# Later feed-forward blocks and three of four down pairs by seven products of quadrants, with GpSimd summing the weight quadrants

## The chip, the cores and the metric

The kernel is one program on one core of a Trainium2 chip. The engines named here are TensorE (PE in the rows, with PEld for its weight loads), VectorE (DVE), ScalarE (ACT), GpSimd (POOL) and the sync engine (SP), which issues most DMAs. The metric is the device time of one execution in microseconds (us). Three runs of the kernel before took 1226.31, 1227.39 and 1228.52 us, median 1227.39.

## What is computed

Two stacked model blocks over 256 tokens of width 1024, all in float32. The first block is feed-forward, then a mixer (differential attention beside an mLSTM), then a second feed-forward. The second block has a gated delta layer and a sparse attention layer. The change touches only the two feed-forward parts and what shares engines with them:

```python
u = modulate(rmsnorm(h, g_ff1), sh1, sc1)             # u: 256 x 1024
h = h + 0.5 * gt1 * ((silu(u @ w1_gate) * (u @ w1_up)) @ w1_down)   # 2816 hidden columns
...
u = modulate(rmsnorm(h, g_ff2), sh3, sc3)
h = h + 0.5 * gt3 * ((silu(u @ w2_gate) * (u @ w2_up)) @ w2_down)
mods = silu(c) @ w_ada + b_ada                        # shifts, scales, gates; also ada_w of block two
```

## The kernel before

Activations lie transposed: `U` and `H` are 128 partitions by 8 chunks of width by 256 tokens. Weights come through a ring `W` of four slots of 2 MB, filled by SP in the order in which they are used. `f1` and `f2` are the two feed-forward parts. The hidden columns of one part are 22 chunks of 128, in 11 blocks of two chunks. For one chunk, `t_gate` issues 16 matrix products (gate and up, 8 chunks of width each) of a 128x128 weight tile with 256 moving columns. In the profile each float32 product appears as two MATMUL records (and two weight loads), so a block of two chunks is 64 records. ScalarE takes the tanh (`s_gate`), VectorE makes the silu and the product (`v_gate`) into `actT`.

The down projection runs over four pairs of output chunks: `t_down` issues 44 products per pair (88 records of 256 columns); the last pair is done in two halves of 128 tokens, so that the next norm can start on half 0. `v_residual` adds the result to `H`.

The first four blocks of `f1` are done as their weights arrive (`t_first_gate`); `t_gate` handles blocks 4 to 10 of `f1`, and all of `f2`. In `f2` block 0 runs in two halves of tokens, since its input `U` comes out of the norm `n3` half by half: `v_root` (reciprocal), `v_normed` (four products H x rstd) and `s_normed` (eight activations) per half.

Beside it VectorE works off the modulation vectors: `v_mod_column` multiplies a 128x1024 tile of the ada weights with the silu of c and sums it (the CUSTOM_DVE rows, ISA in the program's order). Groups of four such tiles come through the same ring `W`, one group per block (`v_ada_blocks`), and `v_ada_mods` adds the bias. Two small extras sit early in `f1`: `t_lambda` and `t_bias` on TensorE; the row of biases is copied by VectorE (`v_bias`) and written to memory by GpSimd (`p_bias`). GpSimd otherwise adds squares for the norms and does nothing during the feed-forward blocks.

Every engine runs its list in order; waits are on counters of the other engines. The order of each list is the order of the calls in `tensor`, `vector`, `scalar`, `gpsimd` and `sync`. A `ring` hands out buffers in turn; `open` waits until the buffer was closed by its last user.

## Time and profile before

| | |
|---|---|
| runs | 1226.31, 1227.39, 1228.52 us |
| profiled execution, span from first to last instruction | 1226.5 us |
| PE busy | 1215.9 us, 99% |
| PEld busy | 1056.1 us, 86% |
| DVE, ACT, POOL busy | 500.7, 297.4, 80.4 us |
| mean granted clock of TensorE | 0.998 |
| chain that ended last | PE 95%, DVE 2%, ACT 1%, DMA 1% |
| HBM | 236.8 MB read, 197 GB/s over the span |

No time of the profiled execution as a whole is recorded beside its span; the span lies 0.9 us under the median of the runs and is taken as its time. A busy share says how long an engine had an instruction in it. Matmuls are pipelined, so that their recorded durations overlap; the pace is read from the starts of neighbouring groups.

### The profile page before, as it was taken

Reading aid. Unit: us, or ns where it says so; the run is one execution under the profiler, and the core shown is the slowest. Engines: PE = TensorE matmul, PEld = TensorE weight load, DVE = VectorE, ACT = ScalarE, POOL = GpSimd, SP = SyncE. Lnnn points to the kernel's source line nnn. Section 1 sums busy time; section 2 is a strip of 40 time slices with the busy share of each in tenths; the row PEclk is TensorE's granted clock in tenths of the full one; section 3 lists DMA queues with packets and bytes.
Section 4 is the critical chain, followed back from the end, with each engine's and each line's share of the span. In section 5 each row is a group of like instructions: output and inputs, shape, how many; then the busy total and the mean of one; then the engine's idle time right before and its main releaser. Section 6 shows DMA issues by size and latency. Waiting matters only on the chain.

```text
span 1226.5 us, 17258 instructions
## 1 busy us (share of the span) xinstructions
PE 1215.9 (99%) x7122; PEld 1056.1 (86%) x7122; DVE 500.7 (41%) x1442; ACT 297.4 (24%) x855; POOL 80.4 (7%) x103
## 2 busy tenths in 40 slices
PE   9999999999999999999999999999999999999997
PEld 7888888996678888889988888898888998888887
DVE  4434440072027533351445442037765322157632
ACT  2110000042124434100300001034424421146542
POOL 0000000000012000011000000030000310000111
PEclk9999999999999999999999999999999999999999
DMA  9968873572475455566888885358242563543311
GB/s 347 336 236 295 308 248 124 205 275 95 151 234 155 174 206 197 183 236 223 278 307 309 309 290 187 105 203 280 78 122 80 187 215 112 153 122 104 104 70 35
DMA packets 163263, 241.52 MB, mean 197 GB/s; under 512 B 13057, under 2 KB 111551, under 8 KB 163184
## 3 DMA queue, kind: packets, MB, share of 16 engines
q1 hardware_dynamic: 155296, 230.45, 55.2%
q10 hardware_dynamic: 6784, 5.74, 1.6%
q0 software_dynamic: 1104, 4.22, 1.0%
q8 instruction: 56, 0.92, 0.3%
q14 instruction: 23, 0.19, 0.0%
HBM read 236.82 MB, written 4.62 MB: 197 GB/s over the span
## 4 chain that ended last, share of the span: by engine, by line
PE 95%; DVE 2%; ACT 1%; DMA 1%; POOL 0%; issue 0%; DVEq 0%; ACTq 0%
PE ps L189 93%; PE ps L192 2%; ACT U L195 1%; DVE tmpB L204 0%; DMA bias_row<-rows 0%; DMA arena<-bias_row 0%; DVE rstd L216 0%; ACT arena L195 0%; ACT tmpC L195 0%; DVE U L198 0%; POOL arena L198 0%; POOL tmpC L198 0%; DVE arena L216 0%; ACT rstd L195 0%; DVE arena L198 0%
## 5 line engine op out<-in xcount | busy, mean ns | idle before, releaser
L189 PE MATMUL ps<-U,slots 128*128 128x256 f32 (+2 forms) x3424 | 700.0, 365 | 0.2 <-DVE arena L198 0.2
L189 PEld LDWEIGHTS ps<-U,slots 128*128 128x128 f32 (+1 forms) x3424 | 601.4, 190 | 78.9 <-issue 5.0
L189 PE MATMUL ps<-arena,slots 128*128 128x256 f32 (+1 forms) x1840 | 324.1, 338 | 0.0
L189 PEld LDWEIGHTS ps<-arena,slots 128*128 128x128 f32 x1840 | 292.5, 191 | 30.1 <-issue 1.8
L207 DVE CUSTOM_DVE_ANT_0 slots<-slots,tmpA 128x1024 f32<-128x1024 f32 x104 | 123.2, 1230 | 5.1 <-DMA slots<-in_w_adaT 4.8
L195 ACT ACTIVATE tmpC<-ps 128x256 f32<-128x256 f32 (+3 forms) x95 | 38.4, 409 | 341.0 <-PE ps L189 334.8
L195 ACT ACTIVATE arena<-ps 128x512 f32<-128x512 f32 (+3 forms) x116 | 50.5, 459 | 153.2 <-PE ps L189 148.9
L204 DVE SCALAR_TENSOR_TENSOR tmpC<-tmpC,ps 128x256 f32<-128x256 f32 (+1 forms) x46 | 18.8, 409 | 149.3 <-ACT tmpC L195 149.3
L195 ACT ACTIVATE tmpC<-H 128x512 f32<-128x512 f32 (+2 forms) x32 | 15.8, 506 | 237.9 <-DVE H L204 195.8
L204 DVE SCALAR_TENSOR_TENSOR H<-ps,sm,H 128x256 f32<-128x256 f32 (+1 forms) x32 | 11.9, 413 | 136.9 <-PE ps L189 136.9
L195 ACT ACTIVATE arena<-arena,st 128x128 f32<-128x128 f32 (+2 forms) x128 | 48.5, 405 | 31.9 <-DVE st L201 31.9
L189 PE MATMUL ps<-arena 128*128 128x128 f32 (+7 forms) x544 | 55.5, 295 | 0.0
L189 PEld LDWEIGHTS ps<-arena 128*128 128x128 f32 (+2 forms) x544 | 47.4, 173 | 8.5 <-issue 4.3
L204 DVE SCALAR_TENSOR_TENSOR tmpB<-arena,hw,tmpB 128x256 f32<-128x256 f32 x96 | 46.5, 485 | 3.4
L195 ACT ACTIVATE U<-U,mods,sm 128x128 f32<-128x128 f32 (+1 forms) x72 | 30.3, 494 | 46.1 <-DVE sm L204 32.1
L195 ACT ACT_TABLE_LOAD x24 | 30.8, 1283 | 10.1 <-DVE tmpB L204 6.4
L207 DVE CUSTOM_DVE_ANT_0 arena<-ps,arena 128x128 f32<-128x128 f32 (+2 forms) x96 | 21.9, 290 | 25.0 <-PE ps L189 24.8
L198 POOL TENSOR_TENSOR arena<-tmpC 128x512 f32<-128x512 f32 x6 | 7.6, 1263 | 350.3 <-ACT tmpC L195 350.3
L204 DVE SCALAR_TENSOR_TENSOR arena<-tmpC,ps 128x512 f32<-128x512 f32 (+1 forms) x18 | 11.3, 631 | 42.0 <-ACT tmpC L195 41.9
L189 PE MATMUL ps<-slots,U 128*128 128x512 f32 x64 | 28.1, 592 | 0.0
L219 DVE COPY arena<-ps 64x256 f32<-64x256 f32 (+2 forms) x16 | 7.3, 457 | 48.9 <-PE ps L189 48.7
L201 DVE TENSOR_SCALAR arena<-arena,st,gates 128x128 f32<-128x128 f32 (+1 forms) x96 | 26.3, 345 | 0.6
(162 smaller groups left out, 747.4 us busy)
## 6 DMA issues: line engine op xcount, KB each, us to landing
slots<-in_w_adaT SPq DMA_DIRECT2D x14, 2048.0 KB, 7.8
slots<-in_w_in SPq DMA_DIRECT2D x14, 2048.0 KB, 9.2
slots<-in_w_down SPq DMA_DIRECT2D x16, 1408.0 KB, 6.6
slots<-in_w_gate SPq DMA_DIRECT2D x18, 1024.0 KB, 5.2
slots<-in_w_up SPq DMA_DIRECT2D x18, 1024.0 KB, 7.9
slots<-in_ada_w1T SPq DMA_DIRECT2D x6, 2048.0 KB, 7.9
slots<-in_ada_w2T SPq DMA_DIRECT2D x6, 2048.0 KB, 8.2
slots<-in_a_in_w SPq DMA_DIRECT2D x6, 2048.0 KB, 10.3
```

The lines of the kernel that those rows point to most:

```text
L189: return Nothing() if self.e is None else self.e.matmul(*a, **k)
L192: return Nothing() if self.e is None else self.e.transpose(*a, **k)
L195: return Nothing() if self.e is None else self.e.activation(*a, **k)
L198: return Nothing() if self.e is None else self.e.tensor_tensor(*a, **k)
L201: return Nothing() if self.e is None else self.e.tensor_scalar(*a, **k)
L204: return Nothing() if self.e is None else self.e.scalar_tensor_tensor(out=o, in0=i0, scalar=s, in1=i1, op0=op0, op1=op1)
L207: return Nothing() if self.e is None else self.e.tensor_tensor_reduce(*a)
L219: return Nothing() if self.e is None else self.e.tensor_copy(*a)
```

## The change

The change computes blocks 5 to 10 of `f1`, blocks 1 to 10 of `f2`, and down pairs 0 to 2 of both parts, by the Winograd form of Strassen's scheme: each matrix product is cut into quadrants (width, weight columns and tokens in halves), and seven products of quadrants, of 128 moving columns each, take the place of eight. That needs sums of quadrants of the weights and of the activations beforehand, and sums of products afterwards.

- `t_gu` on TensorE: seven products p1, p2, p6, p5, p7, p3, p4, each for gate and up, 4 chunks of width, 128 tokens: 56 products of 128 columns for a block in place of 32 of 256. `t_dn`: 7 x 11 = 77 in place of 44 for a pair.
- `p_t` on GpSimd: the four weight sums t1 to t4 of a block, 1024 elements per partition each. t1, t2, t4 go to a ring of two sets (`TG`); t3 overwrites a quadrant of the weight slot. p6 waits for t2, p7 for t3, p4 for t4.
- `p_dn_t` on GpSimd: three sums of 1408 elements for a down pair; the fourth (`v_dn_t1`) is VectorE's.
- `v_su` and `v_sd` on VectorE: the four sums of the activations (of `U`, once for each part, and of `actT`).
- Running sums: ScalarE copies the products' partial sums out of PSUM (s1, u2, s5, u3, c21); VectorE adds (`v_gu`, `v_dn`); then tanh, silu and product on a whole block at once (`s_gu_tanh`, `v_gu_act`).
- The ada tiles no longer go through `W` but through a ring `AR` of four single tiles of 0.5 MB in the arena, loaded by `fetch_chunk`: three a block for most blocks, four for each of the down pairs. The weights of `f1` block b+1 (`f2` block b+2) stand on SP's queue beside the tiles of block b.
- `p_bias` stays at the head of GpSimd's list, ahead of the first `p_t`; `v_bias` now comes right after `v_gate(9)`. The squares' sums move from the arena to `ABT`; rope's load moves into the norm `n2`. `tmpB` and `tmpC` become parts of one tile `tmps`, the PSUM banks parts of one tensor `ps`.

```diff
             for b in range(4, 11):
-                fetch("ada", b)
                 if b < 10:
                     fetch("f1 gu", b + 1)
-            for h in range(8):
-                fetch("f1 dn", h)
+                for g, c in CHUNKS["f1"].get(b, ()):
+                    fetch_chunk(g, c)
+            for p in range(4):
...
+            fetch("f2 gu", 0)
+            fetch("f2 gu", 1)
+            e.wait_ge(*pe.at("pb", 3))
             for b in range(11):
-                fetch("f2 gu", b)
-                fetch("ada", 18 + b)
-            for h in range(8):
-                fetch("f2 dn", h)
+                for g, c in CHUNKS["f2"].get(b, ()):
+                    fetch_chunk(g, c)
+                if b < 9:
+                    fetch("f2 gu", b + 2)
...
+        AR = ring(*[arena[:, 5632 + 1024 * i:6656 + 1024 * i] for i in range(4)])
+        CHUNKS = {"f1": {}, "f2": {}}
+        for f, g0, counts in (("f1", 4, {4: 3, 5: 3, 6: 3, 7: 3, 8: 2, 9: 2}),
+                              ("f2", 18, {0: 3, 1: 4, 2: 3, 3: 3, 4: 3, 5: 3, 6: 3, 7: 3, 8: 3})):
...
+        SETS = [(psum[:, i:i + 2, :], psum[:, i + 2:i + 4, :]) for i in (4, 0)]
+        Q = ring(*SETS)
...
+        TG = ring(*[arena[:, 9728 + 3072 * i:12800 + 3072 * i].rearrange("p (t n k c) -> p t n k c", t=3, n=2, k=4) for i in range(2)])
...
+        def v_su(e, f, tag):
...
+            a11, a12, a21, a22 = (U[:, 4 * k:4 * k + 4, HALF[h]] for h in range(2) for k in range(2))
+            e.tensor_tensor(SU[0], a21, a22, ALU.add).then_inc(*dve.up())
+            e.tensor_tensor(SU[2], a11, a21, ALU.subtract).then_inc(*dve.up())
+            e.wait_ge(*dve.now())
+            e.tensor_tensor(SU[1], SU[0], a11, ALU.subtract).then_inc(*dve.up())
+            e.wait_ge(*dve.now())
+            e.tensor_tensor(SU[3], a12, SU[1], ALU.subtract).then_inc(*dve.up("su", f))
+        def p_t(e, f, b):
+            t, free = TG.open(f, b)
+            for x in free:
+                e.wait_ge(*x)
+            w = gu_block(f, b)
+            e.wait_ge(*arrived(f + " gu", b))
+            e.tensor_tensor(t[:, 0], w[:, :, 0:4, P:T], w[:, :, 0:4, 0:P], ALU.subtract).then_inc(*pool.up(f, "t1", b))
+            e.wait_ge(*pool.at(f, "t1", b))
+            e.tensor_tensor(t[:, 1], w[:, :, 4:8, P:T], t[:, 0], ALU.subtract).then_inc(*pool.up(f, "t2", b))
+            e.tensor_tensor(w[:, :, 0:4, P:T], w[:, :, 4:8, P:T], w[:, :, 0:4, P:T], ALU.subtract).then_inc(*pool.up(f, "t3", b))
+            e.wait_ge(*pool.at(f, "t2", b))
+            e.tensor_tensor(t[:, 2], w[:, :, 4:8, 0:P], t[:, 1], ALU.subtract).then_inc(*pool.up(f, "t4", b))
+        def t_gu(e, f, b):
+            (A, C2), free = Q.open(f, b)
+            for x in free:
+                e.wait_ge(*x)
+            w, t = gu_block(f, b), TG.buf(f, b)
...
+            e.wait_ge(*dve.at("su", f))
+            e.wait_ge(*pool.at(f, "t2", b))
+            e.wait_ge(*act.at(f, "s1", b))
+            for n in range(2):
+                i = product(A[:, n, 0:P], t[:, 1, n], SU[1], False)
...
+            e.wait_ge(*pool.at(f, "t3", b))
+            e.wait_ge(*act.at(f, "u2", b))
+            for n in range(2):
+                i = product(A[:, n, 0:P], w[:, n, 0:4, P:T], SU[2], False)
+            i.then_inc(*pe.up(f, "p7", b))
...
+            W.close([pe.now(), pool.at(f, "t4", b)], f + " gu", b)
+            e.wait_ge(*pool.at(f, "t4", b))
+            e.wait_ge(*act.at(f, "u3", b))
+            for n in range(2):
+                i = product(A[:, n, 0:P], t[:, 2, n], U[:, 4:8, HALF[1]], False)
+            i.then_inc(*pe.up(f, "p4", b))
+            TG.close([pe.now()], f, b)
...
+            e.activation(E[:, :, 1, :], A, ACT.Copy).then_inc(*act.up(f, "u2", b))
...
+            if b - 1 >= (5 if f == "f1" else 1):
+                e.wait_ge(*dve.at(f, "c22", b - 1))
+            e.wait_ge(*pe.at(f, "p7", b))
+            e.activation(FG, A, ACT.Copy).then_inc(*act.up(f, "u3", b))
+            e.wait_ge(*pe.at(f, "p4", b))
+            e.activation(x_[:, 1, :, 0, :], A, ACT.Copy).then_inc(*act.up(f, "c21", b))
+        def v_gu(e, f, b):
+            (A, C2) = Q.buf(f, b)
+            E, x_ = EG.buf(f, b), XG.buf(f, b)
+            e.wait_ge(*act.at(f, "u2", b))
+            e.wait_ge(*act.at(f, "s5", b))
+            e.wait_ge(*pe.at(f, "p3", b))
+            e.tensor_tensor(x_[:, 0].rearrange("p n j t -> p n (j t)"), C2[:, :, 0:T], E.rearrange("p n j t -> p n (j t)"), ALU.add).then_inc(*dve.up(f, "c1", b))
+            e.wait_ge(*act.at(f, "u3", b))
+            e.tensor_tensor(x_[:, 1, :, 1, :], x_[:, 1, :, 1, :], FG, ALU.add).then_inc(*dve.up(f, "c22", b))
+        def s_gu_tanh(e, f, b):
+            E, x_ = EG.buf(f, b), XG.buf(f, b)
+            th = E.rearrange("p h j t -> p h (j t)")
+            e.wait_ge(*dve.at(f, "c22", b))
+            e.wait_ge(*act.now())
+            e.activation(th, x_[:, :, 0].rearrange("p h j t -> p h (j t)"), ACT.Tanh, scale=0.5).then_inc(*act.up(f, "th", b))
+        def v_gu_act(e, f, b):
+            E, x_ = EG.buf(f, b), XG.buf(f, b)
+            th = E.rearrange("p h j t -> p h (j t)")
+            e.wait_ge(*act.at(f, "th", b))
+            e.stt(th, th, 1.0, x_[:, :, 0].rearrange("p h j t -> p h (j t)"), ALU.add, ALU.mult).then_inc(*dve.up())
+            e.wait_ge(*dve.now())
+            to = actT[:, 2 * b:2 * b + 2, :].rearrange("p j (h t) -> p h j t", h=2)
+            e.tensor_tensor(to, E, x_[:, :, 1], ALU.mult).then_inc(*dve.up())
+            dve.mark(f, "act", 2 * b)
+            dve.mark(f, "act", 2 * b + 1)
+            EG.close([dve.now()], f, b)
+            XG.close([dve.now()], f, b)
...
+        def v_sd(e, f, k0, k1):
+            a11, a12, a21, a22 = (actT[:, 11 * k + k0:11 * k + k1, HALF[h]] for h in range(2) for k in range(2))
+            s1, s2, s3, s4 = (SD[:, n, k0:k1, :] for n in range(4))
+            e.wait_ge(*dve.at(f, "act", 10 + k1))
+            e.tensor_tensor(s1, a21, a22, ALU.add).then_inc(*dve.up())
+            e.tensor_tensor(s3, a11, a21, ALU.subtract).then_inc(*dve.up())
+            e.wait_ge(*dve.now())
+            e.tensor_tensor(s2, s1, a11, ALU.subtract).then_inc(*dve.up())
+            e.wait_ge(*dve.now())
+            e.tensor_tensor(s4, a12, s2, ALU.subtract).then_inc(*dve.up())
...
+        def v_dn_t1(e, f, p):
+            lo, hi = dn_of(f, p)
+            e.wait_ge(*(pe.at(f, "p4", 9) if p == 0 else pe.at(f, "p4", 10) if p == 1 else pe.at(f + " dn", "p4", 0)))
+            e.wait_ge(*arrived(f + " dn", 2 * p))
+            e.tensor_tensor(TD[3 * p % 4], lo[:, :, P:T], lo[:, :, 0:P], ALU.subtract).then_inc(*dve.up(f + " dn", "t1", p))
+        def p_dn_t(e, f, p):
+            lo, hi = dn_of(f, p)
+            t1, t2, t4 = (TD[(3 * p + n) % 4] for n in range(3))
+            e.wait_ge(*dve.at(f + " dn", "t1", p))
+            e.wait_ge(*arrived(f + " dn", 2 * p + 1))
+            if p:
+                e.wait_ge(*pe.at(f + " dn", "p5", p - 1))
+            e.tensor_tensor(t2, hi[:, :, P:T], t1, ALU.subtract).then_inc(*pool.up(f + " dn", "t2", p))
+            e.tensor_tensor(lo[:, :, P:T], hi[:, :, P:T], lo[:, :, P:T], ALU.subtract).then_inc(*pool.up(f + " dn", "t3", p))
+            e.wait_ge(*(pe.at(f + " dn", "p6", p - 1) if p else pe.at(f, "p4", 10)))
+            e.wait_ge(*pool.at(f + " dn", "t2", p))
+            e.tensor_tensor(t4, hi[:, :, 0:P], t2, ALU.subtract).then_inc(*pool.up(f + " dn", "t4", p))
...
+            product(A[:, 0:P], lo[:, :, 0:P], actT[:, 0:11, HALF[0]], True, 0).then_inc(*pe.up(n, "p1", p))
+            e.wait_ge(*arrived(n, 2 * p + 1))
+            product(C2[:, 0:P], hi[:, :, 0:P], actT[:, 11:22, HALF[0]], True, 11).then_inc(*pe.up(n, "p2", p))
+            e.wait_ge(*dve.at("sd", f))
+            e.wait_ge(*pool.at(n, "t2", p))
+            e.wait_ge(*act.at(n, "s1", p))
+            product(A[:, 0:P], t2, SD[:, 1], False).then_inc(*pe.up(n, "p6", p))
+            product(C2[:, P:T], t1, SD[:, 0], False).then_inc(*pe.up(n, "p5", p))
...
+            for p in range(3):
+                t_dn(e, f, p)
+            for x in free_of(Q, 1):
+                e.wait_ge(*x)
+            t_down(e, f, 3, 0)
+            t_down(e, f, 3, 1, amid={(1, 0): first_sums})
...
+            t_gate(e, "f1", 8, "n1")
+            t_gate(e, "f1", 9, "n1")
+            t_lambda(e)
+            t_bias(e)
+            for x in free_of(S, 1) + free_of(X):
+                e.wait_ge(*x)
+            t_gu(e, "f1", 5)
+            for x in free_of(L) + free_of(S):
+                e.wait_ge(*x)
+            for b in range(6, 11):
+                t_gu(e, "f1", b)
+            t_downs(e, "f1", "n2")
...
+        def v_gu_blocks(e, f, b0):
+            for b in range(b0, 11):
+                if b > b0:
+                    v_gu_act(e, f, b - 1)
+                chunks = CHUNKS[f].get(b, [])
+                v_ada_chunks(e, chunks[:2])
+                if b == 10:
+                    v_sd(e, f, 0, 9)
+                    v_dn_t1(e, f, 0)
+                v_ada_chunks(e, chunks[2:])
+                v_gu(e, f, b)
+            v_gu_act(e, f, 10)
+            v_sd(e, f, 9, 11)
...
+            v_su(e, "f1", "n1")
+            v_gate(e, "f1", 8)
+            v_gate(e, "f1", 9)
+            v_bias(e)
+            v_ada_chunks(e, CHUNKS["f1"][4])
+            v_gu_blocks(e, "f1", 5)
...
         def gpsimd(e):
             p_bias(e)
+            for b in range(5, 11):
+                p_t(e, "f1", b)
+            for p in range(3):
+                p_dn_t(e, "f1", p)
...
+            e.wait_ge(*pe.at("sums", "n3", 1))
+            e.wait_ge(*pool.now())
+            for b in range(1, 11):
+                p_t(e, "f2", b)
+            for p in range(3):
+                p_dn_t(e, "f2", p)
```

The order on two engines. GpSimd's list, from its first work on, before (names: `bias_row` is memory, `tmpC` and `arena` scratch):

```order
L225 DMA bias_row<-tmpB 16x384
L198 ISA
L198 TENSOR_TENSOR arena<-tmpC 128x512
L198 TENSOR_TENSOR arena<-arena,tmpC 128x512
L198 TENSOR_TENSOR arena<-arena 128x256
```

And now, for the first block with seven products and the start of the third (`slots` are weights, `s_products` is TensorE's counter):

```order
L225 DMA bias_row<-tmps 16x384 [waits s_vector_results]
L198 ISA
L198 TENSOR_TENSOR arena<-slots 128x1024 [waits s_slot0]
L198 TENSOR_TENSOR arena<-slots,arena 128x1024 [waits s_pool_results]
L198 TENSOR_TENSOR slots<-slots 128x2x4x128
L198 TENSOR_TENSOR arena<-slots,arena 128x1024 [waits s_pool_results]
...
L198 TENSOR_TENSOR arena<-slots 128x1024 [waits s_slot2,s_products]
```

The sums of the weights stand between the DMA of the bias row and the work that was GpSimd's first; from the third block on the first of four waits for TensorE.

VectorE's list for a block of `f1` before: two `v_gate` (here the second) and four ada tiles (ISA rows):

```order
L204 SCALAR_TENSOR_TENSOR tmpC<-tmpC,ps 128x256 [waits s_scalar_results]
L198 TENSOR_TENSOR arena<-tmpC,ps 128x256 [waits s_vector_results]
L207 ISA slots,mods<-slots,tmpA 128x1024 [waits s_slot0]
L207 ISA mods 128x1
L207 ISA slots,mods<-slots,tmpA 128x1024
L207 ISA mods 128x1
```

And now, around block 6: `v_gu(5)`, `v_gu_act(5)`, then three ada tiles, the first shown whole:

```order
L198 TENSOR_TENSOR tmps<-ps,tmps 128x512 [waits s_products,s_scalar_results]
L198 TENSOR_TENSOR tmps<-tmps,rstd 128x2x128 [waits s_scalar_results]
L204 SCALAR_TENSOR_TENSOR tmps<-tmps 128x512 [waits s_scalar_results]
L198 TENSOR_TENSOR arena<-tmps 128x2x2x128 [waits s_vector_results]
L207 ISA arena,mods<-arena,tmpA 128x1024 [waits s_ada_chunk2]
L207 ISA mods 128x1
```

Before, each `v_gate` row has one input in PSUM (`ps`). Now three of the four rows of a block take both inputs from SBUF, and the ada tiles stand between the activation of one block and the sums of the next.

## Rows read from the trace of the kernel before

**Rows 1.** The page: busy time, and the chain that ended last by engine.

```profile
PE 1215.9 (99%) x7122; PEld 1056.1 (86%) x7122; DVE 500.7 (41%) x1442; ACT 297.4 (24%) x855; POOL 80.4 (7%) x103
PE 95%; DVE 2%; ACT 1%; DMA 1%; POOL 0%; issue 0%; DVEq 0%; ACTq 0%
```

**Rows 2.** Busy time in windows; window, length, engines (instructions), clock, DMA share, GB/s.

```profile
89.00:103.00 14.00, 14.00 (x65) 11.94 (x65) 6.40 (x13) 0.48 (x3) 0.00 (x0) 1.00 0.86 300
229.00:249.00 20.00, 20.00 (x178) 19.90 (x177) 3.87 (x9) 3.74 (x9) 2.90 (x4) 1.00 0.56 211
```

**Rows 3.** Timeline of TensorE: start, length, instruction, shape, records.

```profile
24.47 1.89 PE L189 MATMUL ps<-U,arena 128*128 128x256 f32 x8
26.20 5.34 PE L189 MATMUL ps<-U,slots 128*128 128x256 f32 x24
...
88.76 14.08 PE L189 MATMUL ps<-U,slots 128*128 128x256 f32 x64
...
172.69 71.88 PE L189 MATMUL ps<-arena,slots 128*128 128x256 f32 x396
...
244.63 5.08 PE L189 MATMUL ps<-arena,slots 128*128 128x128 f32 x44
249.54 3.74 PE L189 MATMUL ps<-U,slots 128*128 128x128 f32 x32
253.11 0.39 PE L189 MATMUL ps<-arena,cst 128*128 128x128 f32 x2
...
738.79 7.50 PE L189 MATMUL ps<-arena,slots 128*128 128x256 f32 x34
```

**Rows 4.** Groups of GpSimd by shape: count, busy us, mean ns, idle before.

```profile
L198 POOL TENSOR_TENSOR arena<-tmpC 128x512 f32<-128x512 f32 x6 | 7.6, 1263 | 350.3 <-ACT tmpC L195 350.3
L198 POOL TENSOR_TENSOR tmpC<-tmpC 128x128 f32<-128x128 f32 x16 | 7.3, 455 | 54.6 <-ACT tmpC L195 54.6
```

**Rows 5.** Timeline of GpSimd, 539 to 551 us.

```profile
539.09 2.18 POOL L198 TENSOR_TENSOR arena<-arena,tmpB 128x512 f32<-128x512 f32 x1 [121.88 <-DVE tmpB L204]
543.94 2.18 POOL L198 TENSOR_TENSOR arena<-arena,tmpB 128x512 f32<-128x512 f32 x1 [2.67 <-DVE tmpB L204]
550.85 1.26 POOL L198 TENSOR_TENSOR arena<-arena,tmpB 128x512 f32<-128x512 f32 x1 [4.72 <-DVE tmpB L204]
```

**Rows 6.** Timeline of VectorE in the same stretch.

```profile
538.93 1.22 DVE L207 CUSTOM_DVE_ANT_0 slots<-slots,tmpA 128x1024 f32<-128x1024 f32 x1
540.07 2.28 DVE L207 CUSTOM_DVE_ANT_0 slots<-slots,tmpA 128x1024 f32<-128x1024 f32 x1
...
545.04 1.10 DVE L198 TENSOR_TENSOR mods<-mods,vec 128x4 f32<-128x4 f32 x1
```

**Rows 7.** Timeline, 955 to 960 us: GpSimd, and VectorE with an input in PSUM.

```profile
955.17 4.96 POOL L198 TENSOR_TENSOR H<-H,arena 128x512 f32<-128x512 f32 x4
...
958.99 0.69 DVE L198 TENSOR_TENSOR arena<-arena,ps 128x512 f32<-128x512 f32 x1 [2.05 <-PE ps L189]
```

**Rows 8.** Timeline, 103 to 105 us: the bias row.

```profile
104.14 0.54 DVE L219 COPY tmpB<-ps 16x384 f32<-16x384 f32 x1
104.99 0.70 POOL L225 DMA_DIRECT2D bias_row<-tmpB  x1 [104.55 <-DVE tmpB L219]
```

**Rows 9.** Timeline, 586 to 600 us: the norm ahead of the second feed-forward.

```profile
589.02 1.07 POOL L225 DMA_DIRECT2D bias_rows<-bias_row  x1
589.46 7.31 PE L189 MATMUL ps<-U,slots 128*128 128x128 f32 x64
590.06 0.95 DVE L216 RECIPROCAL rstd<-rstd 128x128 f32<-128x128 f32 x1 [4.20 <-ACT rstd L195]
591.05 1.43 DVE L198 TENSOR_TENSOR U<-H,rstd 128x256 f32<-128x256 f32 x4
591.51 3.19 ACT L195 ACTIVATE U<-U,mods,sm 128x128 f32<-128x128 f32 x8 [1.48 <-DVE U L198]
596.98 3.28 PE L189 MATMUL ps<-U,slots 128*128 128x128 f32 x27 [0.21 <-DVE arena L198]
```

**Rows 10.** Window at the end of the program, with TensorE mostly idle.

```profile
1216.00:1226.00 10.00, 4.06 (x35) 3.68 (x33) 4.65 (x8) 2.20 (x8) 0.00 (x0) 0.81 0.34 105
```

268 lines of the change are left out of this document (212 added, 56 removed).

## The prediction

> **What bounds the kernel now.** First the page: TensorE is busy 99% of the span and makes up 95% of the chain that ended last; VectorE is busy 41%, GpSimd 7% [rows 1]. So time is won only by less work on TensorE, as long as nothing else becomes late. Then the windows: in a 14 us stretch of gate/up blocks TensorE has no gap, VectorE works 6.4 us, GpSimd nothing; in a stretch of 128-column products the weight loads are as full as the products, 19.90 of 20.00 us [rows 2]. Then the timeline, for the pace: 8 records of 256 columns from 24.47 to 26.20, 216 ns each; 76 records of 128 columns from 244.63 to 253.11, 111.6 ns each, not 108 [rows 3]. Last, the timelines of GpSimd and VectorE side by side, because the change gives both much work at once: there stands the price that the diff does not show [rows 5, 6].
>
> **TensorE's work.** A gate/up block is 64 records at 216 ns = 13.8 us before and 112 at 111.6 ns = 12.5 us after; 16 blocks save 16 x 1.32 = 21.2 us. A down pair is 88 x 216 ns = 19.0 us before and 154 x 111.6 ns = 17.2 us after; 6 pairs save 10.9 us. Together 32 us of TensorE time: that is all there is to win.
>
> **GpSimd's work.** 128 elements take 455 ns and 512 take 1263 ns [rows 4], so 2.10 ns an element and 0.19 us fixed. A sum of 1024 elements is then 2.34 us, four of them 9.4 us a block; a sum of 1408 is 3.15 us, three of them 9.5 us a pair. Alone, this fits under 12.5 and 17.2 us.
>
> **The two engines exclude each other.** At 539.09 GpSimd starts a sum of 512 elements while VectorE is in an ada tile. It takes 2.18 us in place of 1.26, and ends 1.20 us after VectorE's tile ended at 540.07 [rows 5, 6]. VectorE's next tile, issued at 540.07, takes 2.28 us in place of 1.22: it started only when GpSimd was through, near 541.13. A sum of 4 elements at 545.04 takes 1.10 us, also behind a sum of GpSimd. The next GpSimd sum, with VectorE free, takes 1.26 us again. Where VectorE has one input in PSUM nothing happens: at 958.99 it takes 0.69 us inside 4.96 us of GpSimd sums that keep 1.24 us each [rows 7]. So VectorE's instructions with two SBUF inputs and GpSimd's sums take turns, each for its whole transfer. Behind these rows stands the Trainium skill, "SBUF — State Buffer", terms and port section: the shared port pair is an exclusive lock held for the full instruction, and the loser fully blocks. By that rule the two loads add up; by shared bandwidth they would hide behind each other, which would give the first rival's time. The trace agrees with the lock.
>
> The hold of a sum of 512 was 540.07 to 541.13, 1.06 to 1.1 us, which is 2.1 ns an element; I take 2.2 us for 1024 and 3.0 for 1408. VectorE holds for 1.08 us per tile (538.93 to 540.07, less 0.06) and about 1.05 ns an element otherwise.
>
> **One block after.** GpSimd 4 x 2.2 = 8.8 us. VectorE with two SBUF inputs: three ada tiles 3.24, c22 of 256 elements 0.27, the two activation steps of 512 elements 1.07, bias sums 0.05: 4.6 us (the sum c1 has PSUM in it and is free). Total 13.4 us of turns. Some ten changes of hand come on top; no row prices them apart, the bounds are 0 (the next is queued) and 0.15 us (GpSimd's fixed part less what overlaps). I take 0.05, an estimate near the lower end, since the engine that waits is already issued: 13.9 us a block, between 13.4 and 14.9. That is above TensorE's 12.5 and level with today's 13.8. What TensorE saves in a block, it waits.
>
> **f1, blocks 5 to 10.** GpSimd's list begins with the bias row's DMA, which waits for VectorE's copy (104.14 to 104.68 today, DMA at 104.99 for 0.70) [rows 8]. In the new order the copy comes after `v_gate(9)`, about 90.3 us, so the sums start at 91.6, while TensorE is ready for block 5 at 89.6 and reaches p6 3.6 us later without t2. From 91.6 on: 24 sums x 2.2 = 52.8; VectorE's turns 16 tiles x 1.08 = 17.3, activations and c22 of five blocks 6.7, four sums of 1152 elements ahead of the downs 4.8, the first down sum 1.5, together 30.3; some 60 changes 3.0. Sum 86.1, so the last t4 is there at 177.7; p4 and the tail of TensorE 2.1: 179.8. Today the downs start at 172.7 [rows 3]. **+7.1 us.**
>
> **f2's norm.** `p_t` of block 1 may start once the norm's sums are taken, and its weights are there. GpSimd is free at 590.1, one us ahead of the first of four normed products of VectorE (591.05 to 592.48), which TensorE's half 1 of block 0 waits for [rows 9]. Each product holds 0.27 us and takes two SBUF inputs. t1 runs to 592.4, then the products alternate with t2, t3, t4: the fourth ends at 592.4 + 0.3 + 3 x (2.2 + 0.3 + 0.1) = 600.5, the last activation of `U` 0.9 later, the product that needs it at 601.8, where it is at 596.8 now. TensorE had only 0.21 us of idle time there. What is queued behind the blocked product is all of VectorE's list, and behind that the activations. **+4.8 us.** Cover that is gone: none. If GpSimd comes 2 us later, it is a little less; bounds 0 and 8.
>
> **f2, blocks 1 to 10.** 10 x 13.9 = 139.0 against 738.8 - 600.6 = 138.2 [rows 3, 9] (596.98 plus the 32 records left of block 0). **+0.8 us**, bounds -4 and +11.
>
> **Downs.** Three pairs of 17.2 are 51.6 us. At the start p6 of pair 0 needs the sums of `actT` with the last block in them: two activation steps and four small sums of VectorE, each of which can meet one of GpSimd's three sums of 3.0 us; that is 9 us of holds and 1.5 of VectorE's, after a tanh 1 us behind p4, while TensorE has p1 and p2, 4.9 us, to do. It waits 10.5 - 4.9 = 5.6 us. Sum 57.2 against 3 x 19.0 = 57.0. Later pairs: 9.0 + 4 tiles 4.3 + 1.5 + 1.5 = 16.3 us of turns, under 17.2. **About 0**, bounds -5 (no wait) and +6, for both parts together -10 and +12.
>
> Moved at no price: v_su (2.1 us of VectorE, hidden behind blocks 0 and 4), the ada tiles as such (same count), ScalarE's five copies of about 0.4 us a block, rope's load.
>
> **Sum.** 7.1 + 4.8 + 0.8 + 0.2 = +12.9 us: 1226.5 -> 1239.4 for the span, and 0.9 more against the median of the runs: **1240 us**. Its own range, from the bounds of a change of hand and of the downs, is 1229 to 1256.
>
> **Rivals.**
> 1. *The port is no limit.* GpSimd and VectorE mostly miss each other. Then TensorE's 32 us come, less about 3 us at block 5: 1198 us. For it: 9.4 us of GpSimd in 12.5. Against it: the three contended rows, all full waits [rows 5, 6].
> 2. *The turns fit.* The holds are as I say, but half of VectorE's turns fall into GpSimd's own pauses (waits for `TG`, for itself), and a block takes 12.9: f1 +2, norm +3, blocks of f2 -9, downs -3: -7, 1220 us. For it: two sets of t buffers are a block of lead. Against it: the turns alone are 13.4.
> 3. *VectorE's chain becomes the bound* (slower than my forecast, and on the other side of before for certain). tanh of block b waits for c22 of b, the next activation for tanh, the tiles come behind it, c22 of b+1 behind those, and u2, on which p7 waits, is behind tanh on ScalarE. Own time of this chain is 7.5 us; where each of four GpSimd sums stops it for its whole hold, 7.5 + 8.8 = 16.3 us a block, 2.4 more than above. It decides once VectorE is more than about 6 us behind TensorE. With 2.4 us on some ten of 16 blocks: 1264 us. SP's list makes it worse: the weights of a later block stand behind tiles whose buffers VectorE must free. A code load of GpSimd's (the ISA row ahead of its first sum) would also fall on the path now; no row prices it.
> 4. *TensorE slows down in its gaps.* With TensorE busy 4.06 of 10 us the granted clock was 0.81 of full, so part of that stretch was at 1.2 GHz [rows 10]. The waits at block 5, at the norm and at the downs are of 5 us each; if each costs 2 us more, 1248 us. It only widens the range.
>
> That the change does not do what it says is no rival of weight: the program's order has the seven products.
>
> **How the numbers follow.** My forecast 0.50 (with rival 4), rival 1 0.12, rival 2 0.18, rival 3 0.20. A difference under 0.2%, 2.5 us, cannot be told from none. Faster: 0.12 + 0.17 + 0.03 of the forecast's lower end = 0.32; same 0.08; slower 0.60. The range for 8 in 10 leaves out most of rival 1 and the far end of rival 3: 1204 to 1264.
>
> **What would show it.** GpSimd's sums of 1024 recorded with a mean near 3 us, not 2.35, and ada tiles well over 1.23: the lock. Block starts in f2 13 to 15 us apart, with TensorE idle before p7 or p6: the turns bound. First p_t at 91 to 92 us, not earlier. The four normed products near 590 spread over 8 us. PEld and PE at 111 to 112 ns a record within products. Wrong it would be if tiles stay at 1.23 us beside GpSimd, if blocks are 12.5 us apart, or if TensorE waits for DMA rather than for `arena` or `tmps`.

## The result, and the profile after

Four runs of the changed kernel took 1258.99 to 1261.04 us, median 1260.55, beside 1227.43 for the kernel before: ratio 1.0266, 95% interval 1.0253 to 1.0279. It is slower by 33 us where 13 were forecast. The profiled execution spans 1258.6 us (1226.5 before).

The page after, busy time and the chain that ended last, against [rows 1]; then TensorE's waits: engine that waits, for whom, total us, times, longest.

```profile
PE 1205.9 (96%) x8286; PEld 1084.5 (86%) x8286; DVE 685.7 (54%) x1496; ACT 330.6 (26%) x943; POOL 322.4 (26%) x185
...
PE 77%; DVE 15%; POOL 2%; ACT 2%; DMA 2%; issue 2%; DVEq 0%; ACTq 0%; POOLq 0%
```

```profile
PE ps L189 <- ACT tmps L195: 20.5, 10, 7.4
PE ps L189 <- DVE arena L198: 11.8, 5, 5.2
PE ps L189 <- POOL arena L198: 7.8, 3, 7.1
PE ps L189 <- ACT U L195: 3.3, 4, 1.3
```

VectorE has come onto the path (15% of the chain). It gained 185 us of busy time; with GpSimd's sums made free (experiment 1) the same 1496 instructions take 552.6 us, so 133 of these are waiting inside an instruction. TensorE's four waits sum to 43.4 us; in the kernel before the same kinds come to 1.5.

Now the groups by shape of GpSimd and VectorE (count, busy us, mean ns, idle before).

```profile
L198 POOL TENSOR_TENSOR arena<-slots,arena 128x1024 f32<-128x1024 f32 x32 | 90.2, 2819 | 1.3
L198 POOL TENSOR_TENSOR slots<-slots 128x1024 f32<-128x1024 f32 x16 | 44.5, 2778 | 0.0
```

```profile
L207 DVE CUSTOM_DVE_ANT_0 arena<-arena,tmpA 128x1024 f32<-128x1024 f32 x88 | 135.0, 1574 | 22.4 <-DMA arena<-in_w_adaT 19.6 <-DMA arena<-in_ada_w1T 2.6
L198 DVE TENSOR_TENSOR arena<-tmps 128x512 f32<-128x512 f32 x16 | 35.0, 2190 | 0.6
L204 DVE SCALAR_TENSOR_TENSOR tmps<-tmps 128x512 f32<-128x512 f32 x16 | 28.4, 1772 | 21.4 <-ACT tmps L195 21.4
L198 DVE TENSOR_TENSOR tmps<-tmps,rstd 128x256 f32<-128x256 f32 x16 | 27.8, 1740 | 0.0
L198 DVE TENSOR_TENSOR tmps<-ps,tmps 128x512 f32<-128x512 f32 x16 | 10.9, 683 | 16.1 <-PE ps L189 16.1
```

A sum of 1024 takes 2.8 us, not 2.34. The activation's two steps of 512 elements take 1.77 and 2.19 us; the one of the same size with an input in PSUM keeps 0.68. That is the lock of [rows 5, 6] against [rows 7], now all through both feed-forward parts.

The ledger by stage, from block and pair starts on TensorE's timeline:

| stage | before | after | change | forecast |
|---|---|---|---|---|
| up to the end of f1's blocks | 172.7 | 183.1 | +10.4 | +7.1 |
| f1 down pairs 0 to 2 | 57.0 | 60.6 | +3.5 | +0.2 |
| f2 norm and block 0 | 11.1 | 18.9 | +7.8 | +4.8 |
| f2 blocks 1 to 10 | 138.2 | 145.0 | +6.8 | +0.8 |
| f2 down pairs 0 to 2 | 57.0 | 60.3 | +3.3 | +0.2 |

The forecast has 57.2 against 57.0 us for the pairs of each part; its sum entered 0.2 for both together, where 0.4 follows. The first row hides a head start. In this execution the row of eight products that starts at 24.47 in [rows 3] starts at 22.39, and block 5 with its first products at 87.43, where 89.6 was forecast:

```profile
87.43 3.84 PE L189 MATMUL ps<-U,slots 128*128 128x128 f32 x32
```

In the experiments, which change nothing on TensorE ahead of this point, block 5 starts between 87.2 and 89.7. That is a difference between executions, and without it the first row would be some +12.5.

From the same starts the length of each of the 16 blocks follows. Seven take 12.5 us, four 13.3 to 13.8, and five 17.6 to 22.6: blocks 5 and 8 of f1, blocks 1, 4 and 9 of f2. The waits are few and long.

Three places in rows. First f1 block 5, all engines on the timeline (start, length, instruction, what the idle time before it ended with).

```profile
89.30 1.21 DVE L207 CUSTOM_DVE_ANT_0 arena<-arena,tmpA 128x1024 f32<-128x1024 f32 x1
89.34 5.66 POOL L198 TENSOR_TENSOR arena<-slots 128x1024 f32<-128x1024 f32 x1
...
90.44 1.21 DVE L207 CUSTOM_DVE_ANT_0 arena<-arena,tmpA 128x1024 f32<-128x1024 f32 x1
...
91.59 1.21 DVE L207 CUSTOM_DVE_ANT_0 arena<-arena,tmpA 128x1024 f32<-128x1024 f32 x1
...
92.84 2.18 DVE L198 TENSOR_TENSOR mods<-mods,vec 128x4 f32<-128x4 f32 x1
...
95.08 3.27 POOL L198 TENSOR_TENSOR arena<-slots,arena 128x1024 f32<-128x1024 f32 x1
...
98.40 6.40 PE L189 MATMUL ps<-ABT,arena 128*128 128x128 f32 x32 [7.14 <-POOL arena L198]
```

GpSimd's first sum was issued at 89.34 and ended at 95.00. It takes 2.35 us when alone, so it ran only from about 92.7, when VectorE's row of tiles had ended; VectorE's sum of 4 elements at 92.84 then waited for it. TensorE waits 7.14 us for t2, and its 32 records after that take 6.40 us, where the same row elsewhere takes 3.74. Second, f1 block 8.

```profile
141.31 3.36 DVE L207 CUSTOM_DVE_ANT_0 arena<-arena,tmpA 128x1024 f32<-128x1024 f32 x1
143.54 3.32 POOL L198 TENSOR_TENSOR slots<-slots 128x1024 f32<-128x1024 f32 x1
...
147.40 2.04 DVE L198 TENSOR_TENSOR tmps<-tmps,rstd 128x256 f32<-128x256 f32 x1
149.47 0.63 ACT L195 ACTIVATE tmps<-tmps 128x512 f32<-128x512 f32 x1 [11.26 <-DVE tmps L198]
...
150.52 3.75 PE L189 MATMUL ps<-ABT,slots 128*128 128x128 f32 x16 [7.43 <-ACT tmps L195]
```

This is the third rival's chain: c22 late on VectorE (147.40), tanh behind it, u2 behind tanh on ScalarE, and p7 waits 7.43 us for u2. What makes c22 late stands ahead of it: three tiles of 3.36 us each, where a tile takes 1.22 alone, so each one waited for a whole sum. Third, the norm of f2, against [rows 9].

```profile
604.08 2.37 POOL L198 TENSOR_TENSOR arena<-slots 128x1024 f32<-128x1024 f32 x1
605.02 9.18 DVE L198 TENSOR_TENSOR U<-H,rstd 128x256 f32<-128x256 f32 x4
...
614.79 2.08 PE L189 MATMUL ps<-U,slots 128*128 128x128 f32 x8 [0.48 <-ACT U L195]
...
617.40 9.89 PE L189 MATMUL ps<-U,slots 128*128 128x128 f32 x64 [0.54 <-DVE arena L198]
...
617.79 4.38 DVE L198 TENSOR_TENSOR ABT<-U 128x512 f32<-128x512 f32 x2
```

The four normed products take 9.18 us in place of 1.43, each behind one of GpSimd's sums. The four sums of U meet GpSimd's sums too: they run from 617.79 to 625.66, 7.9 us where the prediction has 2.1 us of own time and no price, and p6 of block 1 then waits 1.96 us. Last, the clock: busy time in windows (window, length, PE, PEld, DVE, ACT, POOL, granted clock, DMA share, GB/s).

```profile
95.00:98.40 3.40, 0.00 (x0) 0.00 (x0) 2.49 (x4) 0.00 (x0) 3.32 (x2) 0.50 1.07 361
98.40:105.00 6.60, 6.60 (x36) 6.60 (x37) 1.04 (x2) 0.46 (x2) 6.60 (x3) 0.59 1.06 382
150.50:154.00 3.50, 3.48 (x16) 3.50 (x17) 3.31 (x6) 0.15 (x1) 0.00 (x0) 0.50 0.91 290
...
105.00:143.00 38.00, 37.47 (x335) 37.21 (x333) 31.86 (x20) 6.33 (x16) 37.69 (x14) 1.00 0.58 196
```

Within the waits the granted clock falls to 0.50, the level of 1.2 GHz, and the products after the wait run at it for a while before they are back at 2.4 GHz. Taking each group of records over its pace of 111.6 ns a record, the slow ones lose 7.9 us in f1 and 13.5 in f2, 21 us together. The mean over the span is 0.975 (0.998 before).

### The profile page after: what moved, and what is told of

Same layout as the page of the kernel before. It is cut to its first block, busy times and chain, and to the rows that moved or that the text cites. A ratio compares the mean times of both kernels' runs of the same rounds, so it can differ in the third digit from the quotient of the medians.

```text
span 1258.6 us, 20000 instructions
## 1 busy us (share of the span) xinstructions
PE 1205.9 (96%) x8286; PEld 1084.5 (86%) x8286; DVE 685.7 (54%) x1496; ACT 330.6 (26%) x943; POOL 322.4 (26%) x185
## 3 DMA queue, kind: packets, MB, share of 16 engines
q10 hardware_dynamic: 6784, 5.74, 1.6%
## 4 chain that ended last, share of the span: by engine, by line
PE 77%; DVE 15%; POOL 2%; ACT 2%; DMA 2%; issue 2%; DVEq 0%; ACTq 0%; POOLq 0%
PE ps L189 75%; DVE arena L207 5%; DVE arena L198 4%; DVE tmps L198 2%; DVE tmps L204 2%; PE ps L192 2%; POOL arena L198 2%; ACT tmps L195 1%; DMA arena<-in_ada_w1T 1%; DVE ABT L198 1%; ACT U L195 0%; DMA bias_row<-rows 0%; DMA arena<-bias_row 0%; DVE rstd L216 0%; ACT arena L195 0%
## 5 line engine op out<-in xcount | busy, mean ns | idle before, releaser
L189 PE MATMUL ps<-U,slots 128*128 128x256 f32 (+2 forms) x2912 | 543.4, 346 | 3.9 <-ACT U L195 3.3
L189 PEld LDWEIGHTS ps<-U,slots 128*128 128x128 f32 (+1 forms) x2912 | 469.9, 192 | 57.1 <-issue 5.4
L189 PE MATMUL ps<-arena,slots 128*128 128x128 f32 (+1 forms) x1840 | 272.6, 308 | 10.3 <-DVE arena L198 10.3
L195 ACT ACTIVATE tmps<-ps 128x256 f32<-128x256 f32 (+2 forms) x151 | 56.4, 381 | 350.9 <-PE ps L189 338.9
L207 DVE CUSTOM_DVE_ANT_0 arena<-arena,tmpA 128x1024 f32<-128x1024 f32 x88 | 135.0, 1574 | 22.4 <-DMA arena<-in_w_adaT 19.6
L198 POOL TENSOR_TENSOR arena<-slots,arena 128x1024 f32<-128x1024 f32 (+1 forms) x44 | 129.2, 2937 | 68.6 <-DVE arena L198 32.3
L189 PE MATMUL ps<-arena 128*128 128x128 f32 (+7 forms) x940 | 106.1, 293 | 1.0 <-DVE arena L198 1.0
L189 PE MATMUL ps<-ABT,arena 128*128 128x128 f32 (+5 forms) x752 | 86.1, 279 | 9.1 <-POOL arena L198 7.1
L189 PEld LDWEIGHTS ps<-ABT,arena 128*128 128x128 f32 (+3 forms) x752 | 76.7, 181 | 10.3 <-POOL arena L198 7.3
L198 POOL TENSOR_TENSOR slots<-slots 128x1024 f32<-128x1024 f32 (+1 forms) x22 | 63.8, 2901 | 0.0
```

Source lines behind the costliest of these rows:

```text
L189: return Nothing() if self.e is None else self.e.matmul(*a, **k)
L195: return Nothing() if self.e is None else self.e.activation(*a, **k)
L198: return Nothing() if self.e is None else self.e.tensor_tensor(*a, **k)
L207: return Nothing() if self.e is None else self.e.tensor_tensor_reduce(*a)
```

## The experiments

All ratios are against the kernel before, from runs on the same chip, with 95% intervals. The experiments ran on several chips, on which the kernel before took 1225.95 to 1227.9 us, so times of different experiments compare to about 2 us. The edits are shortened: counter increments, and the moves of buffers and waits that an edit brings with it, are left out. Unless said otherwise the edits are made to the changed kernel (1260.55 us).

**1. The sums cut to 1 of 128 columns.**

```diff
-e.tensor_tensor(t[:, 0], w[:, :, 0:4, P:T], w[:, :, 0:4, 0:P], ALU.subtract)
+e.tensor_tensor(t[:, 0, :, :, 0:1], w[:, :, 0:4, P:P + 1], w[:, :, 0:4, 0:1], ALU.subtract)
... (t2, t3, t4 and the down pairs' sums alike)
```

> GpSimd's weight sums of the gate/up blocks and of the down pairs are cut to 1 of every 128 columns (the weight sums are left out, so the products with sums work on stale numbers; every instruction, wait and DMA stays). Theory A (GpSimd and VectorE shut each other out, and all of TensorE's waits come from that): the waits of 5 to 7 us before p6 and p7 of blocks 5, 8, 4 and 9 go, the clock stays at 2.4 GHz through both stages, and TensorE's 32 us come through: 1226 + 1 - 32 = about 1196 us (1192 to 1204). Theory B (VectorE's chain c22, tanh, activation, tiles is too long by itself, or SP's list order starves the blocks): the gate/up blocks still take 14 us or more each and the time stays above 1225 us.

1201.01 us beside 1225.95 for the kernel before, ratio 0.979 (0.9771 to 0.981), as theory A said. TensorE's saving is real, the f1 downs take 51.6 us, and of the large waits one is left, 3.00 us at block 5 with 3 us of slow products behind it. Timeline of GpSimd there:

```profile
91.35 3.53 POOL L198 TENSOR_TENSOR arena<-slots 128x8 f32<-128x8 f32 x1
```

An addition of 8 elements takes 3.53 us: it ends at 94.88, just behind the last of VectorE's row of tiles. Theory B falls.

**2. Throwaway products in TensorE's waits.**

```diff
+fill(e, C2[:, 0, 384:512], w, FILL6.get((f, b), 0))        # before p6: f1 b5: 28, f2 b1: 10
 e.wait_ge(*dve.at("su", f))
...
+fill(e, Q.buf(f, b - 1)[0][:, 0, 384:512], w, FILL7[f, b]) # before p7: f1 b8: 28, f2 b4: 14, b9: 12
 e.wait_ge(*pool.at(f, "t3", b))
```

> Adds throwaway products on TensorE (128 x 128 x 128, into PSUM columns that nobody reads) just where TensorE waits: 28 before p6 of f1 block 5, 28 before p7 of f1 block 8, 10 before p6 of f2 block 1, 14 and 12 before p7 of f2 blocks 4 and 9, 12 in block 0 of f2, 20 before the 20th activation row in the downs of both parts. They shorten no wait; they keep TensorE busy in it. Theory C (of the 32 us that the changed kernel is behind, some 19 are products run at 1.2 GHz after a wait): granted clock over the span from 0.975 back to above 0.99, and 8 to 16 us faster than the changed kernel, 1244 to 1252 us. Theory D (the waits alone cost the time; TensorE's slower pace after them is absorbed by the next wait): no change or slower by what the fills overrun, 1260 to 1268 us.

1252.65 us, ratio 1.0216 (1.0192 to 1.0239), with more work on TensorE: 8 us faster than the changed kernel by the medians, 6 by the ratios. The four runs spread from 1250.72 to 1256.1. Mean granted clock 0.993. The timeline of TensorE:

```profile
100.65 3.84 PE L189 MATMUL ps<-ABT,arena 128*128 128x128 f32 x32 [0.91 <-POOL arena L198]
150.47 2.02 PE L189 MATMUL ps<-ABT,slots 128*128 128x128 f32 x16 [1.19 <-ACT tmps L195]
...
624.82 5.44 PE L189 MATMUL ps<-ABT,arena 128*128 128x128 f32 x32 [2.17 <-ACT tmps L195]
```

Behind the filled waits of f1 the products are back at 3.84 and 2.02 us (6.40 and 3.75 unfilled). The slow pace lost falls from 21.4 to 6.4 us. Where TensorE is the bound after the wait, this comes through: f1's blocks take 91.3 us (95.7), its downs 58.3 (60.6), 6.7 us together. In f2 it does not: p6 of block 1 starts 25.8 us after the norm's products in both kernels (599.02 to 624.82 here, 603.44 to 629.25 there), because VectorE's normed products and U sums, and the silu of c behind them, end no earlier. From there to the downs both take 138 us; where block 4's wait is filled, block 5 waits 3.14 us instead. In f2's downs the filler did not hold the clock: the 44 records behind the wait take 6.80 us (7.19 unfilled, 5.08 at full clock). Theory C holds for f1, theory D for f2's norm and blocks; for f2's downs this run does not decide.

**3. GpSimd starts f2's sums after the last normed product.**

```diff
-e.wait_ge(*pe.at("sums", "n3", 1))
+e.wait_ge(*dve.at("un", "n3", 3, 1))
```

> GpSimd's weight sums for f2 block 1 (and all behind them) start after the last normed product of VectorE instead of after the statistics' sums. Theory A (the sums shut VectorE out of its four normed products, U comes late): the stretch 603.4 to 622.3 of the changed kernel (18.9 us against 11.1 before) shrinks by 5 to 8 us; the sums of block 1 then end some 3 us later and p6 of block 1 may wait 2 to 5 us, so -2 to -7 us in all: 1253 to 1259 us. Rival (the late U comes from ScalarE's normed parts or from the clock): no change within 1 us.

1260.45 us, ratio 1.0268 (1.0249 to 1.0287): nothing gained, where theory A expected 2 to 7 us. The products take 1.43 us again, and the next work of VectorE with two SBUF inputs is hit in their place (timeline of VectorE and TensorE):

```profile
606.17 1.43 DVE L198 TENSOR_TENSOR U<-H,rstd 128x256 f32<-128x256 f32 x4
...
612.49 5.60 DVE L198 TENSOR_TENSOR ABT<-U 128x512 f32<-128x512 f32 x2
...
629.64 5.83 PE L189 MATMUL ps<-ABT,arena 128*128 128x128 f32 x32 [10.13 <-ACT tmps L195]
```

**4. A small operation of GpSimd's at the start of the program.**

```diff
+e.memset(pw[:, :], 1.0)
+e.tensor_tensor(pw[:, 0:8], pw[:, 8:16], pw[:, 8:16], ALU.add)
 p_bias(e)
```

> A memset and one addition of 8 columns on a tile of their own at the head of GpSimd's work, at the start of the kernel. Theory E (GpSimd's first sum at 89.34 took 5.66 us because its code was loaded in it for some 3.4 us): the first sum then takes 2.2 to 3 us in the place and TensorE's wait of 7.14 us before p6 of block 5 shrinks by 3 us or more, with the clock behind it 4 to 6 us: 1254 to 1257 us. Rival F (VectorE's back-to-back tiles keep the port until 92.7, GpSimd only waits for it): the first sum stays at 5 us or more and the time does not change.

1260.16 us, ratio 1.0276 (1.0256 to 1.0297), and the first sum still takes 5.74 us. An earlier operation of the same kind changes nothing, so theory E falls and rival F fits.

```profile
90.68 5.74 POOL L198 TENSOR_TENSOR arena<-slots 128x1024 f32<-128x1024 f32 x1
```

**5. VectorE's tiles cut to 8 of 1024 elements.**

```diff
-v_mod_column(e, AR.buf(g, c), mod_col(g) + c)
+e.tensor_tensor_reduce(w[:, 0:8], w[:, 0:8], CR[:, 0:8], 0.5, 0.0, ALU.mult, ALU.add, mods[:, col:col + 1])
```

> VectorE's modulation tiles are cut to 8 of 1024 elements in the feed-forward stages (their sums are left out, so the modulation is wrong; every DMA, wait and order stays). VectorE loses some 1.1 us for each of 31 tiles of f1 and 44 of f2 and no longer keeps GpSimd out with them. Theory A (GpSimd's sums and VectorE's tiles shut each other out, and the waits of 5 to 7 us come from it): nearly the same as the run with narrow sums, 1198 to 1210 us. Rival G (of VectorE's work it is not the tiles but its activations, U sums and normed products that meet the sums, or SP's order of the weights): gate/up blocks 5 to 10 of f1 speed up only to 90 us and f2 stays above 160 us: 1235 to 1250 us.

1231.01 us, ratio 1.0032 (1.002 to 1.0045). The answer lies between: the tiles carry 30 of 60 us of the distance to free sums, the norm, the U sums and the down pairs (waits of 5.16 us in both parts) the other half. For the gate/up blocks alone theory A is right: all blocks but the first with seven products in each part take 12.5 us, without a wait.

**6. The tiles take the silu of c from PSUM.**

```diff
+e.tensor_copy(CP, CR)                    # CP: two PSUM banks, freed by packing each block's sums into one bank
-v_mod_column(...)                       # that is e.tensor_tensor_reduce(w, w, CR, 0.5, ...)
+e.tensor_tensor_reduce(w, w, CP, 0.5, ...)
```

> The silu of c is copied to PSUM once per part and VectorE's modulation tiles take it from there, so that a tile has one input in SBUF; every tile and every sum is still computed. Theory A2 (what shuts GpSimd out is an operation of VectorE with two inputs in SBUF, as the 0.69 us of an addition with a PSUM input during a GpSimd operation of 4.96 us suggests): tiles take 1.1 to 1.3 us beside a running sum, the first weight sum ends by 92 instead of 95, the f1 gate/up stage falls from 95.7 to 80 to 86 us, f2's from 145 to 135 to 140, and the time to 1225 to 1240 us. Rival H (GpSimd and VectorE's tiles contend whatever the source, or a PSUM source makes the tile itself slower): tiles of 3 us remain and the time is 1255 us or more.

1230.3 us, ratio 1.003 (1.0019 to 1.004), with all the work done. Tiles and sums run beside each other on the timeline:

```profile
90.50 2.38 POOL L198 TENSOR_TENSOR arena<-slots 128x1024 f32<-128x1024 f32 x1
90.86 1.22 DVE L207 CUSTOM_DVE_ANT_0 arena<-arena,ps 128x1024 f32<-128x1024 f32 x1
...
92.95 2.36 POOL L198 TENSOR_TENSOR arena<-slots,arena 128x1024 f32<-128x1024 f32 x1
```

68 tiles now average 1212 ns (four at the end of f2, and all outside the feed-forward parts, still take both inputs from SBUF). The time is that of run 5, which left the PSUM banks alone, so the packing of the banks is not what gained. As there, all blocks but the first with seven products take 12.5 us in both parts, although the activation's two steps still meet the sums (means 1.89 and 2.44 us). What is left besides the norm is the end of f1's blocks, where a pair's sums meet the activation of block 10:

```profile
166.09 3.17 POOL L198 TENSOR_TENSOR arena<-slots,arena 128x1408 f32<-128x1408 f32 x1 [13.59 <-DVE arena L198]
...
166.53 3.02 DVE L198 TENSOR_TENSOR tmps<-tmps,rstd 128x256 f32<-128x256 f32 x1
...
170.24 2.87 DVE L204 SCALAR_TENSOR_TENSOR tmps<-tmps 128x512 f32<-128x512 f32 x1 [0.70 <-ACT tmps L195]
...
173.15 3.52 DVE L198 TENSOR_TENSOR arena<-tmps 128x512 f32<-128x512 f32 x1
...
176.72 1.23 PE L189 MATMUL ps<-arena,slots 128*128 128x128 f32 x4 [5.16 <-DVE arena L198]
```

**7. Plain down pairs.** In `t_downs`, `vector`, `scalar` and `gpsimd` the calls for pairs 0 to 2 are those of the kernel before:

```diff
-t_dn(e, f, p)
+t_down(e, f, p, to=DP)      # DP: banks 4 to 6
```

> All down pairs as in the kernel before, by plain products; the gate/up blocks stay in seven products. It tells the share of the down pairs: from the trace they cost 3.5 us in f1 and 3.3 us in f2 (60.6 and 60.3 us against 57.0), with some 4.5 us of TensorE at the low clock behind a wait of 5.2 us for the activations. Theory I (the pairs' own sums and waits cost that): both stages at 57 to 58 us, -5 to -7 us: 1253 to 1256 us. Rival J (the wait of 5.2 us comes from the gate/up blocks' backlog on VectorE and stays with plain pairs): 60 us each and no change, 1259 to 1262 us.

1252.04 us, ratio 1.0205 (1.019 to 1.0221); the f1 pairs take 71.88 us for all but the last half, as in [rows 3], and start without a wait. Theory I, and a little more than it said.

**8. Weights ahead of the tiles on SP's list in f2.**

```diff
 for b in range(11):
+    if b < 9:
+        fetch("f2 gu", b + 2)
     for g, c in CHUNKS["f2"].get(b, ()):
         fetch_chunk(g, c)
-    if b < 9:
-        fetch("f2 gu", b + 2)
```

> On SP's list the weights of gate/up block b + 2 of f2 are fetched ahead of the modulation tiles of block b, not behind them. Theory K (GpSimd's wait of 19.6 us for block 3's weights loses its lead, and the waits of 3.7 us at block 4 and 3.2 us at block 9 follow from it): both waits go, with the slow clock behind them -5 to -10 us: 1251 to 1256 us. Rival L (the waits are those of VectorE's and ScalarE's chain, which the lock lengthens, not GpSimd's lead; tiles that come later only move them): within 2 us of 1260.5.

1259.57 us, ratio 1.0265 (1.025 to 1.0281): rival L. A wait of 3.14 us now stands one block later than the 3.69 of before, another of 3.14 in the same block as the 3.15.

**9. As 6, the sums of pair 0 after block 10's activation.**

```diff
-e.wait_ge(*dve.at(f + " dn", "t1", p))
+e.wait_ge(*(dve.at(f, "act", 20) if p == 0 else dve.at(f + " dn", "t1", p)))
```

> The c-from-PSUM kernel, and GpSimd's weight sums for down pair 0 wait for the activation of block 10 in both parts. In the c-from-PSUM kernel they ran from 166.09 to 176.1 beside the activation of block 10, of which two additions and a product took 3.02, 2.87 and 3.52 us, and TensorE waited 5.16 us for them in f1 and 4.42 in f2. Theory M (that meeting makes the wait): the wait for the activation falls to about 0.5 us or none, the sums then are late for p6 of pair 0 by 2 to 4 us, so -2 to -4 us per part with the slow clock: 1222 to 1227 us. Rival N (the later sums cost as much as they free): 1229 to 1232 us.

1231.64 us, ratio 1.0036 (1.0022 to 1.0051): rival N. The activation is free, and VectorE's four small sums behind it take 10.29 us:

```profile
171.10 10.29 DVE L198 TENSOR_TENSOR arena<-arena 128x256 f32<-128x256 f32 x4
...
181.45 6.94 PE L189 MATMUL ps<-arena 128*128 128x128 f32 x44 [8.06 <-DVE arena L198]
```

**10. As 9, f2 block 1 plain, sums behind the U sums, weights ahead of tiles.**

> As the run before it, and in f2 block 1 is plain again, GpSimd's sums begin with block 2 and after VectorE's sums of U (so neither the normed products nor the sums of U meet them), and gate/up weights are fetched ahead of modulation tiles. The f2 norm and block 0 fall from 18.9 to 11 to 12 us, the wait before p6 of block 1 (2.1 us and 1.6 of slow clock) goes, and a plain block costs 1.3 us more: another -8 to -10 us, 1213 to 1219 us, below the kernel before (1227). If the sums for block 2 come late, or the modulation tiles that now start some 5 us later hold SP's list, 1220 us or more.

1238.43 us, ratio 1.0095 (1.0079 to 1.0111): a miss. The norm is cured (block 1 ends 25.5 us after the products with the norm's sums start, 35.1 in experiment 11), but the tiles start after block 1's activation, behind weights on SP's list, and one arrives late; c22 stands behind it, and p7 of block 3 waits. The run changes several things at once and does not price them one by one:

```profile
637.64 1.22 DVE L207 CUSTOM_DVE_ANT_0 arena<-arena,ps 128x1024 f32<-128x1024 f32 x1 [6.96 <-DMA arena<-in_ada_w1T]
...
647.21 3.40 PE L189 MATMUL ps<-ABT,slots 128*128 128x128 f32 x16 [10.45 <-ACT tmps L195]
```

**11. As 6, with plain down pairs.**

> The c-from-PSUM kernel with all down pairs by plain products, as in the kernel before. It tells what the seven-product pairs are worth once the tiles don't meet the sums: the f1 downs took 60.2 us in the c-from-PSUM kernel and 57.0 plain, so -3 us per part: 1223 to 1226 us. If the wait for block 10's activation is not made by the pairs' own sums, it stays and the time is 1228 us or more.

1222.31 us, ratio 0.9959 (0.9945 to 0.9973), as expected and the first below the kernel before: the wait goes with the pairs' own sums.

**12. As 11, f2 block 1 plain in banks 3 and 2, tiles ahead of its activation, sums behind the U sums.**

> The c-from-PSUM kernel with plain down pairs, and in f2 block 1 plain too (in two PSUM banks of its own, with the modulation tiles ahead of its activation), GpSimd's sums beginning with block 2 and behind VectorE's sums of U. Theory A (of the 18.9 us that the norm and block 0 of f2 took, 8 are GpSimd's sums shutting VectorE out): the norm and block 0 return to 11 us, the wait before the first p6 to 0 to 1 us, the plain block costs 1.3: -6 to -8 us from 1222.3: 1214 to 1217 us. Rival O (as in the run that fetched the weights first, the tiles come late and a wait of 10 us moves to block 3): 1222 to 1232 us.

1214.23 us, ratio 0.989 (0.9873 to 0.9906), as theory A said. The normed products take 1.43 us and block 0's second half waits 0.21:

```profile
588.99 1.43 DVE L198 TENSOR_TENSOR U<-H,rstd 128x256 f32<-128x256 f32 x4
...
594.91 21.23 PE L189 MATMUL ps<-U,slots 128*128 128x128 f32 x128 [0.21 <-DVE arena L198]
```

**13. As 12, block 5's sums ahead of the bias row.**

```diff
+e.wait_ge(*dve.at("su", "f1"))
+p_t(e, "f1", 5)
 p_bias(e)
-for b in range(5, 11):
+for b in range(6, 11):
```

> As the run before it, and GpSimd's four sums for f1 block 5 start right behind VectorE's sums of U (at 79 us, when block 5's weights have landed) instead of behind the bias row (at 90.5). The wait of 2.96 us before p6 of f1 block 5 and the slow clock behind it (up to 2.7 us) go, -3 to -6 us: 1209 to 1213 us. If the bias row's DMA is late for the first copy of block 5, nothing or 1 us is gained.

1208.0 us, ratio 0.9841 (0.9827 to 0.9856), 1 us better than expected. The first sum starts at 79.44 and takes 2.35 us; p6 of block 5 starts at 92.70 with no wait.

**14. As 13, with the three seven-product pairs.**

> As the run before it but with three of four down pairs in seven products, as the change has them. It tells again what these pairs are worth when all else meets nothing: the wait of 5.2 and 4.4 us for block 10's activation stays, so +7 to +8 us against the run before it (as 1230.3 against 1222.3). If the wait was fed by the backlog of the blocks ahead, it shrinks and the pairs gain: 3 us or more faster than the run before it.

1217.57 us, ratio 0.9919 (0.9904 to 0.9934), 9.6 us behind 13. The waits of 5.16 and 4.41 us are as in 6, so they do not come from a backlog; the loss is 1.6 us more than the expected 8.

**15. As 14, pair 0 plain, pairs 1 and 2 in seven products, their sums behind VectorE's.**

```diff
-for p in range(3):
+t_down(e, f, 0, to=DP)      # DP: bank 3
+for p in (1, 2):
     t_dn(e, f, p)
```

> As the run with early sums of block 5 and seven-product pairs, but pair 0 of the downs is plain and only pairs 1 and 2 take seven products; GpSimd's sums for pair 1 start behind VectorE's sums of the activations. Theory P (the seven-product pairs lose because the first of them needs block 10's activation after 20 short products, 2.2 us, while the pair's own sums hold that activation up; under a plain pair 0 of 14.3 us both are covered): no wait over 1 us in the downs, each part's downs 53 to 54 us against 57.0 plain and 60 with three pairs: -6 to -8 us against the plain-pair run of 1208: 1200 to 1203 us. Rival Q (two sums of U, the tiles and the pairs' sums still meet and a wait of some us moves to pair 1): 1206 to 1214 us.

1201.47 us, ratio 0.9789 (0.9776 to 0.9802), as theory P said and the best of all, 26 us below the kernel before and 59 below the changed one. The downs take 53.4 us in each part. Its windows of f1's blocks and downs (columns as above):

```profile
88.00:163.00 75.00, 75.00 (x664) 74.01 (x663) 55.60 (x64) 14.79 (x36) 51.74 (x22) 1.00 0.84 285
163.00:220.00 57.00, 57.00 (x431) 54.73 (x430) 35.24 (x53) 6.39 (x15) 20.74 (x8) 1.00 0.70 233
```

TensorE has no gap there and the clock stays at 2.4 GHz. The saving is what is left of the 32 us: less 3.6 for two pairs and 1.3 for one block that are plain again, 27; measured 26.

## Why the prediction was right in kind and wrong in size

**What TensorE saves** was right: with free sums (run 1) 25 of the 32 us come through, and the one wait left, with the slow products behind it, is 6 of the other 7; in run 15 the count of products gives the time to about 1 us.

**The lock** was right, in kind and price: sums near 3 us, normed products spread over 9 us (forecast 8), activation steps and tiles well over their own time, and it goes when the second input lies in PSUM (run 6, -30 us). Behind it stands the rule of the Trainium skill that the prediction named ("SBUF — State Buffer", the terms): the loser blocks for the whole instruction. The trace agrees: a tile of 1.22 us takes 3.36 behind a sum.

**The waits as a total** were right, by stage too. The forecast's +12.9 over a saving of 32 means 45 us of waits; the trace has 43.4 less the 1.5 that were there before, 42. For f1's blocks the forecast has 15.0 (its 7.1 and the 7.9 saved) and the trace 15.1, for the norm 4.8 and 3.9, for f2's blocks 14.0 and 11.3, for the downs 5.6 and 5.7 in each part. Part of this is luck, because the waits do not come as forecast. The forecast spread them over all blocks, 13.9 us each; seven of the 16 blocks take 12.5 us, which the prediction itself gave as a sign of being wrong, and five take most of the waits.

**The step that failed is the clock**, the fourth rival, of which the prediction said "It only widens the range" and left it out of the sum. On TensorE's timeline the products at 1.2 GHz behind the waits cost 21 us: 42 of waits and 21 of slow pace less the 32 saved are 31 of the 32.1 us between the spans. As a price it is less, since a later wait takes part of it up. Filling the waits took 15 of the 21 away and gave back 8 us by the medians, 6 by the ratios, 7 by the stages, nearly all of it in f1. That is about the 8 us that the fourth rival gave as its own price, 2 at each of four waits; the error was to leave them out. So 6 to 8 us of the miss (20.5 by the medians, 19.2 by the spans) are shown to be the clock's. The f1 pairs' excess over the forecast of 57.2, 3.3 us, is the 3.0 us of slow records behind their wait. The like 2.8 us in f2's pairs were not tested, since the filler there did not hold the clock. In f2's norm and blocks the slow pace is no cost of its own.

**The second part of the miss is f2's norm and blocks**, 9 us over the forecast (+7.8 for +4.8 and +6.8 for +0.8). At the norm the prediction moved the sums of U "at no price", hidden behind blocks 0 and 4. In f2 they took 7.9 us behind GpSimd's sums, and p6 of block 1 waits behind them (run 3 moves the meeting wholly onto them; run 12 takes both away). The blocks' 145.0 us are 14.5 a block, inside the bounds of 13.4 to 14.9 and above the 13.9 that was taken. The third rival's chain, c22, tanh, u2, p7, is what TensorE waits for there: 9.4 us in f2 and 8.0 in f1, at seven blocks, but over 2.4 us at only three, not at ten of 16. Its mark of a code load fell with run 4, that of SP's order with run 8. It was given 0.20 and is a part of the truth. What lengthens the chain most are the tiles' turns: with the tiles cut (run 5) or reading from PSUM (run 6) no p7 waits in either part, although the activation steps stay slow. How much a change of hand costs, for which the forecast took 0.05 us, the runs do not show.

**The downs at "about 0"** named the right wait and left out what it triggers. The pair's own sums hold up the very activation that the pair waits for: moving them behind it only moves the wait (run 9), and it goes with other work for TensorE in between (run 15) or without the sums (run 11).

## What to carry to other kernels

Before work is moved to GpSimd, list what VectorE has with two inputs in SBUF in the same stretch, and move one input of the longest of these to PSUM: here that alone was worth 30 us. A wait of TensorE is priced with the slow products behind it wherever TensorE stays the bound (2 to 3 us for a wait of 5 to 7; a wait of 3 us cost 3 us more in run 1 and nothing in run 6). Work that fits by totals needs cover at the seams too: one plain pair at the start of the downs cost 1.8 us of TensorE's saving and removed a wait of 5 us and the slow products behind it; one plain block at the start of f2, with GpSimd's sums begun behind the sums of U, cost 1.3 us and gave 8 net.

## What the runs showed of the hardware

- VectorE's tiles, issued one behind the other, kept a waiting GpSimd operation out over three of them: 5.66 us for a sum of 2.35 in the changed kernel, 5.74 in run 4, and 3.53 us for an addition of 8 elements in run 1. Two of the three tiles (90.44, 91.59) started after the sum was issued (89.34). So here the engine that waited first was not served first; in the rows that follow the two take turns.
- A small operation waits as long as a large one: VectorE's sum of 4 elements took 2.18 us behind a GpSimd sum (0.16 free, in run 9).
- A tile with one input in PSUM takes 1.22 us, as from SBUF (1.23), and runs beside a sum of 2.38 us (2.35 alone) with next to no loss to either (run 6).
- After a wait of 7 us the granted clock was at 1.2 GHz, and 32 records took 6.40 us for 3.74; with filler products in the wait, 3.84 (run 2). After waits of 3 us both were seen: 6.76 us for such a row after 3.00 in run 1, at 0.50, and 3.84 after 2.95 in run 6, at 1.00.
